# One queue's order at the opening of an MLP's down phase: loads of h and of weights in turn

## The chip, the cores and the metric

The kernel runs on one core of a Trainium2 chip. The metric is the device time of one execution in microseconds, the median of several runs. Three runs of the kernel before gave 2327.13, 2330.32 and 2327.13 us, so the median is 2327.13 us.

## What is computed

The reference is one inference step of a two-layer decoder (model width 1024, MLP width 4096, 1024 prompt tokens and 8 x 4 sample tokens, 1056 in all, all float32): an mLSTM layer and then a sliding-window attention layer. Each of the two ends in the MLP that this case is about:

```
def sq_relu_mlp(x, w_up, w_down):
    h = jax.nn.relu(x @ w_up)
    return (h * h) @ w_down
...
        x = x + sq_relu_mlp(rmsnorm(x, norm_ffn[l]), w_up[l], w_down[l])
```

## The kernel before

All five engines run instruction streams written by hand, tied together by semaphores. Each float32 operand of a matmul is split into a high part (ScalarE, a copy that rounds) and a low part (VectorE, the operand minus its high part), and three matmuls (high by high, high by low, low by high) make one product.

**The MLP.** The function `mlp` stands once for each engine, and `mlp_loads` (L777) is SyncE's part, the only one that issues the DMAs of weights and of h. The MLP's 4096 hidden rows are 16 blocks (NF) of 256. The up phase makes a block of h at a time and stores it to DRAM (`store_h`, L794). The down phase multiplies by w_down with a seven-product scheme (Strassen's, in a variant): the table DOWN names for each of the 7 products which half of the weights is summed with which other half, and which half of h with which other. A product runs over 7 groups (KG), so q runs from 0 to 48 (NG is 49), and a short tail follows (NW is 53 weight slabs). A group q is four pairs of output banks by 12 matmuls, 48 matmuls of 128x264 in all (L2765 to L2767).

**What a group needs.** `load_w(q)` (L803) loads a slab of weights into one of three places in turn (`w_raw`, `w_raw_odd`, `w_third`), and in the first product a second slab into one of two others; POOL adds the two (`down_sum`, L1499); ACT makes the high part (`w_high`, L1067); DVE makes the low part (`w_low`, L1669); only then may PE run group q. `load_h(q)` loads the group's part of h: for q = 0 to 6 into its own place in `b11` (L839), for q = 7 to 13 into `b21_even` or `b21_odd` (L848). ACT makes its high part (`t_high_of`, L1084) and DVE its low part (`t_low_of`, L1677), one group ahead of the weights.

**Waits ahead of the loads.** load_w(1) waits for the last split of the up phase (`op_lo`), load_w(2) for the store of block 14 (`h_stored`), load_w(q) from q = 3 for the low part of the weights of group q - 3 (`dw_lo`). The second slab of load_w(q) waits for POOL's sum of group q - 2 (`dw_sum`, L823, issue at L824). The first four h loads wait for a product of the up phase, and from the fifth on load_h(q) waits for the landing of load_h(q - 4) (`db_loaded`, L838). `store_h(15)` waits for the last two halves of h (`scaled`, L1663), which are worked out while the down phase is already under way; ACT's `stage` at the end of product 0 waits for this store, since it writes over the place where those halves lie.

**The order at the opening.** Each engine takes its instructions in the order in which they are written. At the end of the up phase DVE's order is: combine C11, U4, C22 (L1656, which read the accumulator), w_low(0), t_low_of(1), C21, C12, scaled(15, 1), w_low(1), t_low_of(2), scaled(15, 0), w_low(2), t_low_of(3) and so on. ACT's order is: t_high_of(0), w_high(0), t_high_of(1), relu and square of one half of block 15 (L1137, L1139), w_high(1), t_high_of(2), relu and square of the other half, w_high(2), t_high_of(3). PE's third and fourth bank pair of group 0 wait for C21 and C12. SyncE's order is the one that the change touches; all h loads of product 0 come first:

```
                for q in range(KG):
                    load_h(q)
                load_w(1)
                load_w(2)
                for q in range(3, NW):
                    if KG <= q + 1 < NG:
                        load_h(q + 1)
                    load_w(q)
                    if q == 4:
                        store_h(NF - 1)
```

Of the kernel before, what the change touches and what calls it, by code (L numbers as in the profile page):

```python
# [206 lines left out]
KG = (NF - TAIL) // 2  # L207
# [9 lines left out]
NG = NPROD * KG  # L217
# [12 lines left out]
def fill_no(layer, f, x):  # L230
    return UP_FILLS * layer + (2 * f + x + 1 if f < PLAIN else 2 * PLAIN + 7 * (f - PLAIN) + x + 1)


def up_no(layer, f, j):
    return UP_STEPS * layer + 7 * (f - PLAIN) + j + 1
# [6 lines left out]
def turns(layer, n, of, ring):  # L242

    return layer * len(range(n % ring, of, ring)) + n // ring + 1
# [6 lines left out]
def build(nc, io):  # L251
    with ExitStack() as ctx:  # L252
# [231 lines left out]
        def down_raw(q):  # L484
            return (w_raw[:, 0], w_raw_odd[:, 0], w_third[:])[q % 3]

        def down_other(n):
            return (w_raw, w_raw_odd)[n % 2][:, 1]
# [8 lines left out]
        def streamed(q):  # L497
            return (b21_even, b21_odd)[STREAMED.index(q) % 2]

        def down_h(q, half):  # L500

            if half == (1, 0):
                return streamed(q)[:]
            return {(0, 0): b11, (0, 1): b12, (1, 1): b22}[half][:, q % KG]
# [185 lines left out]
        def _(sp):  # L690
# [86 lines left out]
            def mlp_loads(layer):  # L777
# [16 lines left out]
                def store_h(f):  # L794
                    for c in (1, 0):
                        sp.wait_ge(zz_ready, 2 * (NF * layer + f) + 2 - c)
                        sp.dma_start(h_rows[layer][2 * f + c], z_of(f)[c]).then_inc(h_stored[f % 2], 16)

                def down_part(f, mh):
                    return down_rows[2 * P * f:2 * P * f + 2 * P, 512 * mh:512 * mh + 512].rearrange("(k p) m -> p k m", p=P)  # L800

                def load_w(q):

                    if q == 0:
                        sp.wait_ge(op_lo, fill_no(layer, NF - 2, 6))
                    elif q == 1:
                        sp.wait_ge(op_lo, fill_no(layer, NF - 1, 6))
                    elif q == 2:
                        sp.wait_ge(h_stored[0], 32 * (NF // 2) * (layer + 1))
                    else:  # L810
                        sp.wait_ge(dw_lo, NW * layer + q - 2)
                    if q < NG:
                        (mh, kh), op, other = DOWN[q // KG][0:3]
                        f = KG * kh + q % KG
                    else:
                        t, mh = TAILS[layer][q - NG]
                        f, op = NF - TAIL + t, None
                    sp.dma_start(down_raw(q).rearrange("p (k m) -> p k m", k=2), down_part(f, mh)).then_inc(dw_loaded[q % 3], 16)
                    if op is not None:
                        n = W_SUMS.index(q)  # L820
                        if n >= 2:
                            sp.wait_ge(dw_sum, len(W_SUMS) * layer + n - 1)
                        mh, kh = other  # L823
                        sp.dma_start(down_other(n).rearrange("p (k m) -> p k m", k=2), down_part(KG * kh + q % KG, mh)  # L824
                                     ).then_inc(dv_loaded[n % 2], 16)

                def load_h(q):

                    i, g = divmod(q, KG)
                    for half in LOADED_IN:  # L830
                        if LOADED_IN[half] == i:
                            n = RESIDENT.index((half, g))
                            kh, nh = half
                            f = KG * kh + g
                            sp.wait_ge(up_done, up_no(layer, NF - 1, (1 if g < 4 else 2) if half == (0, 0) else 6))
                            sp.wait_ge(h_stored[f % 2], 32 * ((NF // 2) * layer + f // 2 + 1))
                            if n >= 4:
                                sp.wait_ge(db_loaded[n % 4], 16 * (turns(layer, n, len(RESIDENT), 4) - 1))  # L838
                            sp.dma_start(down_h(q, half), h_rows[layer][2 * f:2 * f + 2, :, HALVES[nh]].rearrange("c p n -> p c n")  # L839
                                         ).then_inc(db_loaded[n % 4], 16)  # L840
                    if q in STREAMED:
                        n, f = STREAMED.index(q), KG + g
                        if n >= 2:
                            sp.wait_ge(dt_sum, len(T_SUMS) * layer + T_SUMS.index(STREAMED[n - 2]) + 1)
                        else:
                            sp.wait_ge(up_done, up_no(layer, NF - 1, 6))
                        sp.wait_ge(h_stored[f % 2], 32 * ((NF // 2) * layer + f // 2 + 1))
                        sp.dma_start(streamed(q)[:], h_rows[layer][2 * f:2 * f + 2, :, FIRST_H].rearrange("c p n -> p c n")  # L848
                                     ).then_inc(ds_loaded[n % 2], 16)

                def load_tail_h():
                    sp.wait_ge(dt_sum, len(T_SUMS) * layer + T_SUMS.index(last_group(3)) + 1)
                    for t in range(TAIL):
                        f = NF - TAIL + t
                        sp.wait_ge(h_stored[f % 2], 32 * (NF // 2) * (layer + 1))
                        for c in range(2):
                            sp.dma_start(h_raw[:, 2 * t + c], h_rows[layer][2 * f + c]).then_inc(ht_loaded, 16)
# [4 lines left out]
                for f in range(1, NF):  # L862
# [2 lines left out]
                        load_up(f + 2)  # L865
                    if f == NF - 2:
                        load_w(0)
                for q in range(KG):
                    load_h(q)
                load_w(1)  # L870
                load_w(2)
                for q in range(3, NW):
                    if KG <= q + 1 < NG:
                        load_h(q + 1)
                    load_w(q)
                    if q == 4:
                        store_h(NF - 1)
                    if q == 4 * KG + 4:
                        load_tail_h()

            mlp_loads(0)

            kv_w = io["w_kv"].rearrange("(k p) m -> p k m", p=P)
# [58 lines left out]
            for p, (kind, n) in enumerate(ATT):  # L942
# [22 lines left out]
                if p == 12:  # L965
                    load_sample_bias(1)
                    load_cache(1)
            mlp_loads(1)
            for t in range(NT):
                sp.wait_ge(yt_dve, t + 1)  # L970
# [2067 lines left out]
```

## Time and profile before

| what | value |
|---|---|
| median of three runs | 2327.13 us |
| the profiled execution | 2330.0 us |
| its span, first to last instruction | 2328.2 us |
| PE busy | 2253.5 us, 97% of the span |
| DVE busy | 1565.2 us, 67% |
| ACT, POOL busy | 1072.2 us, 46%; 501.8 us, 22% |
| granted TensorE clock, mean | 0.99 |

The profile is of one execution, 2.9 us above the median and inside the spread of the three runs. Times in the rows are microseconds from the start of the span unless a view says ns. PE is TensorE's matmuls, DVE VectorE, ACT ScalarE, POOL GpSimd, SPq the queue of SyncE, which issues the DMAs. Layer 0's MLP opens its down phase near 897 us and layer 1's near 1957 us.

### The profile page before, as it was taken

The page shows a single profiled execution, that of the slowest core. Times are in us where ns is not written, and L with a number is a line of the kernel's source. Part 1 is how long each engine was busy: PE and PEld are TensorE (multiplying, and loading weights), DVE is VectorE, ACT ScalarE, POOL GpSimd, SP SyncE. Part 2 cuts the span into 40 slices and gives each one's busy share as a digit, 9 for nine tenths or more (in the row PEclk, how much of TensorE's full clock was granted, in tenths as well). Part 3 has the DMA queues.
Part 4 walks back from the last instruction along what each step waited for, and adds up shares of the span by engine and source line. Part 5 has one row for each costly group of instructions (what it writes and reads, how often), then busy time and mean ns, then how long its engine had stood idle before and what let it go on. Part 6 is the DMA issues. An engine that isn't in the chain of part 4 may idle for free. (4 is left out here: it accounts for less than half of the span.)

```text
span 2328.2 us, 41472 instructions
## 1 busy us (share of the span) xinstructions
PE 2253.5 (97%) x16886; PEld 2151.6 (92%) x16886; DVE 1565.2 (67%) x2516; ACT 1072.2 (46%) x2058; POOL 501.8 (22%) x403
## 2 busy tenths in 40 slices
PE   8999999999999999999999999999999999999999
PEld 7989898888999999999999877869999999999998
DVE  7555555569765556788976666475855656798883
ACT  4233222245766664433423454254666664343435
POOL 1000000013222223113412011013122223123323
PEclk9999999999999999999999999999999999999999
DMA  4111121102233336655641312101233336665551
GB/s 131 37 51 57 50 70 41 41 25 65 93 97 107 111 111 239 229 193 200 197 140 49 97 32 53 31 16 46 83 104 110 109 95 224 226 224 188 181 174 75
DMA packets 220928, 256.28 MB, mean 110 GB/s; under 512 B 27687, under 2 KB 144340, under 8 KB 220708
## 3 DMA queue, kind: packets, MB, share of 16 engines
q1 hardware_dynamic: 220596, 253.61, 33.6%
q8 instruction: 135, 2.21, 0.4%
q14 instruction: 53, 0.43, 0.1%
q10 hardware_dynamic: 144, 0.02, 0.0%
HBM read 211.84 MB, written 46.93 MB: 111 GB/s over the span
## 5 line engine op out<-in xcount | busy, mean ns | idle before, releaser
L2765 PE MATMUL acc<-t_hi,w_hi 128*128 128x264 f32 x1568 | 450.5, 287 | 24.5 <-DVE w_lo L1669 24.5
L2766 PE MATMUL acc<-t_lo,w_hi 128*128 128x264 f32 x1568 | 450.8, 287 | 0.0
L2767 PE MATMUL acc<-t_hi,w_lo 128*128 128x264 f32 x1568 | 450.6, 287 | 0.0
L2765 PEld LDWEIGHTS acc<-t_hi,w_hi 128*128 128x128 f32 x1568 | 299.9, 191 | 27.9 <-DVE w_lo L1669 27.9
L2767 PEld LDWEIGHTS acc<-t_hi,w_lo 128*128 128x128 f32 x1568 | 298.7, 190 | 0.0
L2766 PEld LDWEIGHTS acc<-t_lo,w_hi 128*128 128x128 f32 x1568 | 298.5, 190 | 0.0
L2731 PE MATMUL acc<-x_lo,w_hi 128*128 128x264 f32 x896 | 254.6, 284 | 0.0
L2732 PE MATMUL acc<-x_hi,w_lo 128*128 128x264 f32 x896 | 254.5, 284 | 0.0
L2730 PE MATMUL acc<-x_hi,w_hi 128*128 128x264 f32 x896 | 254.4, 284 | 0.0
L2486 PE MATMUL acc<-x_hi,w_hi 128*128 128x352 f32 x576 | 193.1, 335 | 1.4 <-DVE pair L1958 1.4
L2730 PE MATMUL acc<-T_hi,w_hi 128*128 128x264 f32 x672 | 190.9, 284 | 0.2
L2731 PE MATMUL acc<-T_lo,w_hi 128*128 128x264 f32 x672 | 190.7, 284 | 0.0
L2732 PE MATMUL acc<-T_hi,w_lo 128*128 128x264 f32 x672 | 190.3, 283 | 0.0
L2488 PE MATMUL acc<-x_hi,w_lo 128*128 128x352 f32 x576 | 185.9, 323 | 0.0
L2487 PE MATMUL acc<-x_lo,w_hi 128*128 128x352 f32 x576 | 185.3, 322 | 0.0
L2730 PEld LDWEIGHTS acc<-x_hi,w_hi 128*128 128x128 f32 x896 | 168.8, 188 | 0.0
L2731 PEld LDWEIGHTS acc<-x_lo,w_hi 128*128 128x128 f32 x896 | 168.7, 188 | 0.0
L2732 PEld LDWEIGHTS acc<-x_hi,w_lo 128*128 128x128 f32 x896 | 168.4, 188 | 0.0
L1677 DVE TENSOR_TENSOR t_lo<-t_sum_of,t_hi 128x1056 fp32r<-128x1056 f32 x70 | 134.6, 1923 | 1.7
L2730 PEld LDWEIGHTS acc<-T_hi,w_hi 128*128 128x128 f32 x672 | 126.6, 188 | 0.7 <-DVE w_lo L1642 0.7
L2731 PEld LDWEIGHTS acc<-T_lo,w_hi 128*128 128x128 f32 x672 | 126.6, 188 | 0.0
L2732 PEld LDWEIGHTS acc<-T_hi,w_lo 128*128 128x128 f32 x672 | 126.1, 188 | 0.0
(396 smaller groups left out, 5700.6 us busy)
## 6 DMA issues: line engine op xcount, KB each, us to landing
w_raw<-in_w_down SPq DMA_DIRECT2D x72, 512.0 KB, 4.9
w_raw_odd<-in_w_down SPq DMA_DIRECT2D x70, 512.0 KB, 4.7
b<-h_rows SPq DMA_DIRECT2D x42, 528.0 KB, 6.1
w_third<-in_w_down SPq DMA_DIRECT2D x34, 512.0 KB, 4.3
h_rows<-z_even SPq DMA_DIRECT2D x32, 528.0 KB, 2.7
w_raw<-in_w_up SPq DMA_DIRECT2D x32, 512.0 KB, 4.5
w_raw_odd<-in_w_up SPq DMA_DIRECT2D x32, 512.0 KB, 5.1
w_raw<-in_w_mlstm_in SPq DMA_DIRECT2D x24, 512.0 KB
```

Source lines behind the costliest of these rows:

```text
L1677: V.tensor_tensor(lo[:], src, hi[:].bitcast(F32), ALU.subtract).then_inc(dt_lo, 1)
L2486: T.matmul(block_of(g), hi, mh[:, span(b)], start=(kk == 0), stop=False)
L2487: T.matmul(block_of(g), hi, ml[:, span(b)], start=False, stop=False)
L2488: x = T.matmul(block_of(g), lo, mh[:, span(b)], start=False, stop=(kk == n_k - 1))
L2730: T.matmul(out[:, q], hi[:, k], mh[:, k, v], start=(k == 0), stop=False)
L2731: T.matmul(out[:, q], hi[:, k], ml[:, k, v], start=False, stop=False)
L2732: x = T.matmul(out[:, q], lo[:, k], mh[:, k, v], start=False, stop=(k == 3))
L2765: T.matmul(out[:, h], hi[:, c, rows], mh[:, c, v], start=(g == 0 and c == 0), stop=False)
L2766: T.matmul(out[:, h], hi[:, c, rows], ml[:, c, v], start=False, stop=False)
L2767: x = T.matmul(out[:, h], lo[:, c, rows], mh[:, c, v], start=False, stop=(g == KG - 1 and c == 1))
```

## The change

SyncE's queue gets another order where the down phase opens, in both layers. h of groups 0 and 1, weights of group 1, h of 2, weights of 2, h of 3 and 4, weights of 3; from there h of group q + 1 and the weights of group q in turn. The store of block 15 of h comes after load_w(5) in place of load_w(4). The loads are the same, each with the waits it had, and no other engine's stream is changed.

```
@@ -865,15 +865,18 @@
                         load_up(f + 2)
                     if f == NF - 2:
                         load_w(0)
-                for q in range(KG):
-                    load_h(q)
+                load_h(0)
+                load_h(1)
                 load_w(1)
+                load_h(2)
                 load_w(2)
+                load_h(3)
+                load_h(4)
                 for q in range(3, NW):
-                    if KG <= q + 1 < NG:
+                    if 4 < q + 1 < NG:
                         load_h(q + 1)
                     load_w(q)
-                    if q == 4:
+                    if q == 5:
                         store_h(NF - 1)
```

## Rows read from the trace of the kernel before

**Rows 1.** PE's waits, whole span: who waited for whom, us, times, longest.
```profile
PE acc L2765 <- DVE w_lo L1669: 24.5, 16, 5.3
```
**Rows 2.** Timeline of PE, layer 0: start, us, engine, line, operation, idle before.
```profile
897.02 0.28 PE L2765 MATMUL acc<-t_hi,w_hi 128*128 128x264 f32 x1
...
902.76 0.28 PE L2767 MATMUL acc<-t_hi,w_lo 128*128 128x264 f32 x1
908.38 0.59 PE L2765 MATMUL acc<-t_hi,w_hi 128*128 128x264 f32 x1 [5.33 <-DVE w_lo L1669]
```
**Rows 3.** Timeline of POOL, layer 0.
```profile
901.89 2.36 POOL L1499 TENSOR_TENSOR w_raw_odd<-w_raw_odd 128x1024 f32<-128x1024 f32 x1 [21.55 <-DMA w_raw_odd<-in_w_down]
904.88 2.35 POOL L1499 TENSOR_TENSOR w_third<-w_third,w_raw 128x1024 f32<-128x1024 f32 x1 [0.63 <-DMA w_raw<-in_w_down]
908.03 2.54 POOL L1499 TENSOR_TENSOR w_raw<-w_raw,w_raw_odd 128x1024 f32<-128x1024 f32 x1 [0.79 <-DMA w_raw_odd<-in_w_down]
914.46 2.95 POOL L1499 TENSOR_TENSOR w_raw_odd<-w_raw_odd,w_raw 128x1024 f32<-128x1024 f32 x1 [3.89 <-DMA w_raw<-in_w_down]
```
**Rows 4.** Timeline of SyncE's queue, layer 0.
```profile
883.69 10.16 SPq L839 DMA_DIRECT2D b<-h_rows  x7
893.90 0.46 SPq L818 DMA_DIRECT2D w_raw_odd<-in_w_down  x1
...
908.76 0.47 SPq L824 DMA_DIRECT2D w_raw<-in_w_down  x1
```
**Rows 5.** Timeline of ACT, layer 0.
```profile
890.76 1.09 ACT L1084 ACTIVATE t_hi<-b 128x1056 fp32r<-128x1056 f32 x1 [4.57 <-DMA b<-h_rows]
...
899.31 1.09 ACT L1139 ACTIVATE act_b<-act_b 128x1056 f32<-128x1056 f32 x1
904.35 1.06 ACT L1067 ACTIVATE w_hi<-w_raw_odd 128x1024 fp32r<-128x1024 f32 x1 [3.95 <-POOL w_raw_odd L1499]
...
916.86 1.06 ACT L1067 ACTIVATE w_hi<-w_raw 128x1024 fp32r<-128x1024 f32 x1 [6.48 <-PE acc L2767]
...
922.73 1.06 ACT L1067 ACTIVATE w_hi<-w_raw_odd 128x1024 fp32r<-128x1024 f32 x1 [3.83 <-PE acc L2767]
```
**Rows 6.** Timeline of DVE, layer 0.
```profile
886.25 0.68 DVE L1642 TENSOR_TENSOR w_lo<-s_tmp,w_hi 128x512 fp32r<-128x512 f32 x1
...
895.15 1.22 DVE L1669 TENSOR_TENSOR w_lo<-w_raw,w_hi 128x1024 fp32r<-128x1024 f32 x1
896.29 1.25 DVE L1677 TENSOR_TENSOR t_lo<-b,t_hi 128x1056 fp32r<-128x1056 f32 x1
897.46 0.70 DVE L1656 TENSOR_TENSOR act_b<-act_b,acc 128x528 f32<-128x528 f32 x1
...
905.44 2.88 DVE L1669 TENSOR_TENSOR w_lo<-w_raw_odd,w_hi 128x1024 fp32r<-128x1024 f32 x1 [3.75 <-ACT w_hi L1067]
908.25 3.44 DVE L1677 TENSOR_TENSOR t_lo<-b,t_hi 128x1056 fp32r<-128x1056 f32 x1
...
913.91 1.25 DVE L1677 TENSOR_TENSOR t_lo<-b,t_hi 128x1056 fp32r<-128x1056 f32 x1
```
**Rows 7.** Stretches of layer 0: busy time by engine, then PEclk, DMA share, GB/s.
```profile
897.00:903.00 6.00, 6.00 (x50) 5.83 (x48) 3.02 (x4) 2.18 (x2) 1.10 (x1) 1.00 1.00 355
...
908.40:911.00 2.60, 2.60 (x12) 2.60 (x13) 2.60 (x1) 1.99 (x3) 2.17 (x1) 0.50 0.51 109
...
1097.90:1101.30 3.40, 3.40 (x17) 3.40 (x17) 3.32 (x4) 1.08 (x1) 0.00 (x0) 0.50 0.84 299
```
**Rows 8.** Timeline of PE, layer 1.
```profile
1957.34 0.28 PE L2765 MATMUL acc<-t_hi,w_hi 128*128 128x264 f32 x1
...
1968.37 0.59 PE L2765 MATMUL acc<-t_hi,w_hi 128*128 128x264 f32 x1 [5.00 <-DVE w_lo L1669]
```
**Rows 9.** Timelines of ACT, DVE and POOL, layer 1.
```profile
1949.07 1.09 ACT L1084 ACTIVATE t_hi<-b 128x1056 fp32r<-128x1056 f32 x1 [2.55 <-DMA b<-h_rows]
...
1976.01 1.06 ACT L1067 ACTIVATE w_hi<-w_raw 128x1024 fp32r<-128x1024 f32 x1 [5.29 <-PE acc L2767]
...
1953.79 1.22 DVE L1669 TENSOR_TENSOR w_lo<-w_raw,w_hi 128x1024 fp32r<-128x1024 f32 x1
...
1962.22 2.36 POOL L1499 TENSOR_TENSOR w_raw_odd<-w_raw_odd 128x1024 f32<-128x1024 f32 x1 [21.56 <-DMA w_raw_odd<-in_w_down]
```
**Rows 10.** Timeline of PE: two later pauses of the same kind, layer 0.
```profile
1096.53 0.39 PE L2765 MATMUL acc<-t_hi,w_hi 128*128 128x264 f32 x1 [2.33 <-DVE w_lo L1669]
...
1190.99 0.39 PE L2765 MATMUL acc<-t_hi,w_hi 128*128 128x264 f32 x1 [0.71 <-DVE w_lo L1669]
```

## Prediction

> **What bounds the kernel now.** I read the page first: PE is busy for 97% of the span, so a change can win only where PE stands still or runs at a lower clock. Then the list of PE's waits over the whole span: matmuls of the down phase waited 24.5 us in 16 pauses for the low part of the weights, and the longest was 5.3 us [rows 1]. PE's timeline places the longest: in layer 0 group 0 runs from 897.02 us, its last matmul starts at 902.76, and group 1 starts only at 908.38, after 5.33 us of idling [rows 2]. Layer 1 has the twin, 5.00 us, ahead of 1968.37 [rows 8]. Both lie where the changed lines act. The other 14 pauses come to 24.5 - 5.3 - 5.0 = 14 us and lie elsewhere.
>
> Followed backward, the pause is a chain. PE waited for w_low(1), 905.44 to 908.32 [rows 6]; that for w_high(1), which started at 904.35 after 3.95 us of waiting for POOL [rows 5]; POOL's sum started at 901.89 and had waited 21.55 us for a DMA [rows 3]; and that load was issued at 893.90, behind seven h loads whose issue had filled the queue from 883.69, 10.16 us [rows 4]. The first of these h loads lands at 890.7 (ACT starts on it at 890.76 [rows 5]), the second weight slab of group 1 at 901.85 (POOL's start [rows 3]). Eight transfers lie between, so one passes each 11.1 / 8 = 1.39 us, while the DMA engines are busy at share 1.00 [rows 7]. They are a line: a slab of weights lands when what stands ahead of it is through. In layer 1 the same reading gives (1962.2 - 1949.05) / 8 = 1.64 us a transfer [rows 9].
>
> **What the pause costs.** Matmuls follow each other at 5.86 / 48 = 0.122 us (group 0: 897.02 to 902.88) [rows 2]. Without the pause group 1 would start at 902.88 and end at 908.74. In fact ACT's w_high(3), released by the end of group 1, starts at 916.86 [rows 5]; the release comes some 0.45 us after the next group could start (an estimate: the last matmul starts 0.12 us before that point and itself takes 0.28, and the signal follows), so group 2 starts at about 916.4. The loss is 916.4 - 908.7 = 7.7 us: 5.5 of standing, 2.2 because the granted clock fell to 0.50 of full, the 1.2 GHz level, after the pause [rows 7]. Layer 1: group 0 from 1957.34, so with 5.87 us a group, the spacing of w_high(3) and w_high(4) [rows 5], group 2 could start at 1957.34 + 2 x 5.87 = 1969.1; it starts at 1976.01 - 0.45 = 1975.55 [rows 8, 9]; the loss is 6.5. Both together, 14.2 us, are the ceiling of the gain.
>
> **The change, part by part.**
>
> *Group 1's weights ahead of five h loads.* In layer 0 SyncE reaches load_w(1) after two h loads, at about 884.6, and waits for the last split of the up phase, done at 886.93 [rows 6]; both slabs are issued by 888, while h of groups 0 and 1 are still moving, so the line never runs dry. They are third and fourth transfers after the first: 890.7 + 3 x 1.39 = 894.9 against 901.85, seven us earlier. Nothing else queued is hurt by the wait of 2.3 us: the h loads behind it are needed from 901 on.
>
> *Where the time goes next.* POOL's sum of group 1 (2.36 us) now falls among DVE's steps. The rows show that two such operations exclude each other: t_low_of from 908.25 took 3.44 in place of 1.25 us, beginning beside a sum that ended at 910.57, and w_low(1) took 2.88 beside the one that ended at 907.23 [rows 3, 6]; the other way round the sum from 914.46 took 2.95, since t_low_of ran until 915.16. Whoever comes second waits until the first is through. The combines (L1656), which read the accumulator, I take as free of it. Replay of layer 0: the sum holds 894.9 to 897.3; w_low(0), which started at 895.15 [rows 6], is pushed behind it and ends at 898.5, so group 0 starts at 898.5, 1.5 late; t_low_of(1) to 899.6, C21 to 900.3; relu and square (2 x 1.09) to 902.5; w_high(1) to 903.5; DVE's scaled half to 903.7 and w_low(1) to 904.9. Group 0 ends at 904.35, group 1 starts at 904.95 and ends at 910.8. The sum of group 3 takes DVE's next turn, 904.9 to 907.3; t_low_of(2) to 908.5, the second scaled half to 909.7, w_low(2) to 910.9. Group 2 starts at 910.95 against 916.4: **gain 5.45**.
>
> Replay of layer 1: the weights land at 1949.05 + 3 x 1.64 = 1954.0, just after w_low(0) has begun at 1953.79 [rows 9], so it is t_low_of(1) that is held, to 1958.5, and group 0 starts on time. C21 to 1959.2, relu and square to 1961.4, w_high(1) to 1962.4, w_low(1) to 1963.8; group 1 1963.9 to 1969.75; the sum of group 3, t_low_of(2), the scaled half and w_low(2) run to 1969.7. Group 2 starts at 1969.8 against 1975.55: **gain 5.75**.
>
> *Clock.* The pauses left are 0.6 to 1.5 us. A pause of 2.33 us was followed by 3.4 us at clock 0.50, half of which, 1.7, is lost [rows 7, 10]; one of 0.71 has matmuls at the usual pace around it. I take 0 for those left; the other bound is 1.7 a layer.
>
> *h loads of groups 2 to 6 and of 7, later.* h(2) is fifth after the first, at 896.3, and needed by ACT at 903.5; h(3) and h(4) by 902; h(5) stands behind the second slab of group 3, whose wait (the sum of group 1) ends by 897.3; h(6) behind load_w(4), which waits for w_low(1) at 904.9: it lands near 911 and is needed near 922. Cost 0, with over 7 us of cover each. If the cover were gone, each late transfer would cost its 1.39.
>
> *store_h(15) one load later.* In the old order it stood ahead of load_w(5) and held it until the second scaled half; now load_w(5) goes first. ACT's stage needs the store only at the end of product 0, over 20 us on. Cost 0, gain 0.
>
> *Downstream.* All later steps wait on one another and on none by the clock, so PE's earlier end passes on. Sum: 5.45 + 5.75 = 11.2 us. Against the profiled execution 2330.0 - 11.2 = 2318.8; it stands 2.9 over the median, so the median becomes 2327.1 - 11.2 = **2316**.
>
> **Rivals.** *A: sums and DVE steps miss one another.* A few tenths decide in layer 0 (894.9 against 895.15), and POOL may take turns that DVE leaves free. Then the whole 14.2 is won: 2313. Against it: 9 us of DVE work and three sums must fit between 895 and 909.
>
> *B: the sum of group 4 comes just ahead of w_low(2).* Its slabs wait for w_low(1) (904.9, 1963.8). In the old order the slab issued at 908.76 was summed at 914.46, 5.6 later [rows 3, 4]; so the sum is ready near 910.9, just behind w_low(2), which starts at 909.7. Were it ready 1.2 us sooner, w_low(2) would wait 2.36 and end at 913; a pause of 2.4 also drops the clock, 1.7 more. That takes 4 us of a layer's gain: 2320 with one layer hit, 2324 with both. The Trainium skill speaks for this one: its page "DMA: Bandwidth & Descriptors", in the part on the cost of a DMA, gives a fixed 2.0 us and 436 KB per us (a fit made on another issuing path); an estimate from it for the two slabs is 2.0 + 1049 / 436 = 4.4 us, ready at 909.3, ahead of w_low(2). By that rule B holds in both layers, 2324; by the row it does not. The 5.6 us of the row decide for me, being the same loads on the same queue.
>
> *C: the change doesn't do what it says.* If the weights still land late, because SyncE stands in one of the waits moved ahead (the split, the store of block 14), nothing moves: 2327. The rows date both waits before 889, against it.
>
> *D: slower.* One mechanism, that of the exclusion, in its worst phase: the sums of groups 1, 3 and 4 each begin just ahead of w_low(0), (1) and (2). Each pushes PE by about 2.3 (1.7 at the first, which has 0.65 of slack), 6.4, and two pauses above 2 us cost 1.7 each: 9.8 a layer against 7.7 and 6.5 removed, so 5.4 slower: 2332.5. It decides only where all three meet; one has to come 1 us sooner and another later than the replay has it.
>
> **How the numbers follow.** Forecast as summed, 2313.5 to 2319: 0.52. A: 0.13. B, one layer or both, or a clock drop with it: 0.22. C, or gains and losses near balance: 0.08. D: 0.05. A measurement here tells about 0.2% (4.7 us) from no change, so faster means below 2322.5: 0.52 + 0.13 + 0.18 of B = 0.83. Same: 0.04 of B + 0.08 = 0.12. Slower 0.05. The range goes from 2311.5 (A, and the runs' own scatter) to 2323.5 (B in both), and leaves out some 0.04 below and 0.14 above.
>
> **What would show it.** PE's timeline should show the two 5 us pauses gone, with at most three pauses of 0.5 to 1.7 us at each opening, and clock 1.00 through 900 to 916. POOL's sum of group 1 should start near 895 and 1955, and DVE should show a stretched w_low(0) in layer 0 (about 3.4 us) and a stretched t_low_of(1) in layer 1. If a pause of over 2 us stands ahead of group 2, B is right; if POOL's sum still starts near 902, C. The later pauses of layer 0 [rows 10] should keep their length and come about 5.5 us sooner; if they grow, the gain is given back there and my step "downstream" is wrong.

## The result, and the profile after

| | kernel before | kernel after |
|---|---|---|
| median of seven runs | 2327.13 us (2322.89 to 2330.83) | 2316.38 us (2310.98 to 2318.28) |
| ratio, 95% interval | | 0.9947 (0.9933 to 0.9961) |
| profiled execution, its span | 2330.0, 2328.2 us | 2310.98, 2309.2 us |
| granted TensorE clock, mean | 0.990 | 0.996 |

The medians differ by 10.75 us; the ratio, made of runs side by side, is 12.3 us, between 9 and 15.6. The forecast was 2316 (2311.5 to 2323.5), faster by 11.2. In the profile after, L2768 is the matmul line that was L2765.

PE's waits over the whole span, the first line of the list (who waited for whom, us, times, longest), answer to [rows 1]:

```profile
PE acc L2768 <- DVE w_lo L1672: 14.3, 15, 2.9
```

24.5 us have become 14.3, and the two pauses of 5 us are gone. The same stretch as [rows 2], PE's timeline of layer 0, and layer 1's for [rows 8]: group 0 starts at 898.25, and no pause stands ahead of group 1. In layer 1 one of 0.37 us is left.

```profile
898.25 0.28 PE L2768 MATMUL acc<-t_hi,w_hi 128*128 128x264 f32 x1
...
1955.11 0.39 PE L2768 MATMUL acc<-t_hi,w_hi 128*128 128x264 f32 x1 [0.37 <-DVE w_lo L1672]
```

SyncE's queue, POOL and DVE of layer 0, for [rows 3, 4, 6]:

```profile
888.20 0.37 SPq L818 DMA_DIRECT2D w_raw_odd<-in_w_down  x1
888.62 0.46 SPq L824 DMA_DIRECT2D w_raw_odd<-in_w_down  x1
889.18 0.41 SPq L839 DMA_DIRECT2D b<-h_rows  x1
...
894.32 2.39 POOL L1502 TENSOR_TENSOR w_raw_odd<-w_raw_odd 128x1024 f32<-128x1024 f32 x1 [12.75 <-DMA w_raw_odd<-in_w_down]
...
909.76 2.44 POOL L1502 TENSOR_TENSOR w_raw_odd<-w_raw_odd,w_raw 128x1024 f32<-128x1024 f32 x1 [2.08 <-DMA w_raw<-in_w_down]
...
894.71 3.08 DVE L1672 TENSOR_TENSOR w_lo<-w_raw,w_hi 128x1024 fp32r<-128x1024 f32 x1
897.72 1.25 DVE L1680 TENSOR_TENSOR t_lo<-b,t_hi 128x1056 fp32r<-128x1056 f32 x1
...
903.03 1.22 DVE L1672 TENSOR_TENSOR w_lo<-w_raw_odd,w_hi 128x1024 fp32r<-128x1024 f32 x1
...
905.87 2.94 DVE L1666 TENSOR_TENSOR act_a<-act_a,rstd 128x1056 f32<-128x1056 f32 x1 [0.45 <-ACT act_a L1142]
908.73 1.21 DVE L1672 TENSOR_TENSOR w_lo<-w_third,w_hi 128x1024 fp32r<-128x1024 f32 x1
```

The weights of group 1 are issued at 888.20, ahead of the third h load, and POOL sums them from 894.32: 3.9 us before group 0 starts, where it was 4.9 us after. The low part of group 0's weights is stretched to 3.08 us beside this sum, as the replay had it. But it ends at 897.79, still 0.46 us before PE is free for it. The low part of group 1 is done at 904.25, within 0.15 us of the end of group 0's matmuls (898.25 + 5.87 = 904.1), so PE meets no visible pause.

ACT's w_high(3), released by the end of group 1, is the measure of the whole opening [rows 5]:

```profile
910.47 1.06 ACT L1070 ACTIVATE w_hi<-w_raw 128x1024 fp32r<-128x1024 f32 x1 [2.71 <-PE acc L2770]
...
1961.27 1.06 ACT L1070 ACTIVATE w_hi<-w_raw 128x1024 fp32r<-128x1024 f32 x1 [2.71 <-PE acc L2770]
```

From group 0's start it comes 910.47 - 898.25 = 12.22 us later in layer 0 (before: 916.86 - 897.02 = 19.84) and 12.55 in layer 1 (before: 18.67). The two openings gave 7.6 + 6.1 = 13.7 us between these two executions. The view of stretches, for [rows 7] (PE, PEld, DVE, ACT, POOL, then PEclk, DMA share, GB/s), shows the clock whole through both groups:

```profile
898.00:904.00 6.00, 6.00 (x52) 6.00 (x50) 4.34 (x5) 4.36 (x5) 2.45 (x1) 1.00 1.04 389
904.00:910.00 6.00, 5.97 (x49) 5.77 (x48) 5.55 (x5) 3.72 (x4) 3.51 (x2) 1.00 0.84 280
```

The spans differ by 19.0 us, more than 13.7. The before profile has five later drops to the 1.2 GHz level, each 3.4 us long and so at most 1.7 us dear: three in the down phases, one at 1418.8 and one at 2319.9. The after profile has none of them, but it reached group 0 of layer 0 1.2 us later. That makes 13.7 + 8.5 - 1.2 = 21.0 us, 2 more than measured, which I can't place. Such drops vary between executions of one kernel (the last experiment), so this part of the difference isn't put down to the change.

### The profile page after: what moved, and what is told of

It reads as the page before. It is cut to its first block and busy times, and to the rows that moved or that the text cites. A ratio compares the mean times of both kernels' runs of the same rounds, so it can differ in the third digit from the quotient of the medians.

```text
span 2309.2 us, 41472 instructions
## 1 busy us (share of the span) xinstructions
PE 2243.8 (97%) x16886; PEld 2141.8 (93%) x16886; DVE 1570.5 (68%) x2516; ACT 1072.1 (46%) x2058; POOL 500.3 (22%) x403
## 5 line engine op out<-in xcount | busy, mean ns | idle before, releaser
L2768 PE MATMUL acc<-t_hi,w_hi 128*128 128x264 f32 x1568 | 446.5, 285 | 14.3 <-DVE w_lo L1672 14.3
L2768 PEld LDWEIGHTS acc<-t_hi,w_hi 128*128 128x128 f32 x1568 | 295.9, 189 | 17.8 <-DVE w_lo L1672 17.7
L1680 DVE TENSOR_TENSOR t_lo<-t_sum_of,t_hi 128x1056 fp32r<-128x1056 f32 x70 | 127.8, 1826 | 1.7
```

Of the source, the lines that this page charges most:

```text
L1680: V.tensor_tensor(lo[:], src, hi[:].bitcast(F32), ALU.subtract).then_inc(dt_lo, 1)
L2768: T.matmul(out[:, h], hi[:, c, rows], mh[:, c, v], start=(g == 0 and c == 0), stop=False)
```

## Experiments

Every one was timed beside the kernel before. A ratio is given with its 95% interval, and as microseconds of 2326. For each opening I read two numbers: the pause ahead of group 1, and the opening's length from group 0's start to w_high(3). Its floor, with PE never waiting, is 11.92 us, found in both layers of the new order without the sums and in layer 1 of the old order without them.

### Group 1's weights alone moved

```
-                for q in range(KG):
-                    load_h(q)
+                load_h(0)
+                load_h(1)
                 load_w(1)
+                for q in range(2, KG):
+                    load_h(q)
                 load_w(2)
```

> Old order, but the weights of group 1 are loaded after the second h; h of 2 to 6 and then the weights of 2 follow, the store of block 15 stays after load_w(4). Line theory (a slab lands when the transfers issued ahead of it are through, 1.39 us each): POOL's sum of group 1 starts near 895 us and near 1953, so the 5 us pauses ahead of group 1 are gone (under 1 us); the sum of group 2 starts near 905 as before, and its weights' low part ends between 909.5 and 911 where group 2 could start at 909, so a pause of 0.7 to 2.3 us stands ahead of group 2 in each layer. Gain against the kernel before 8 to 12 us (the whole change: 10.8). Rival (only the store's place or the later loads matter): the pause ahead of group 1 stays at 5 us, gain 0.

Measured 0.9973 (0.9964 to 0.9983), 6.3 us gained, median 2320.34. The pauses ahead of group 1 are 0.32 and 0.36 us. Those ahead of group 2 came as forecast: PE's timeline in both layers, and POOL's second sum, which started only at 903.10 after 7.27 us of waiting for its load.

```profile
903.10 2.52 POOL L1501 TENSOR_TENSOR w_third<-w_third,w_raw 128x1024 f32<-128x1024 f32 x1 [7.27 <-DMA w_raw<-in_w_down]
...
911.31 0.39 PE L2767 MATMUL acc<-t_hi,w_hi 128*128 128x264 f32 x1 [1.75 <-DVE w_lo L1671]
...
1965.16 0.39 PE L2767 MATMUL acc<-t_hi,w_hi 128*128 128x264 f32 x1 [1.73 <-DVE w_lo L1671]
```

The pause follows the slab that is left behind the h loads. The gain, 6.3, lies under the 8 to 12 expected. Up to w_high(4), which comes after this pause, the two openings are 2.4 and 2.0 us longer than in the kernel after, 4.4 of the 6.0 us by which the gain falls short of the whole change's; the rest is within the intervals. No drop of the clock stands behind these pauses of 1.7 us.

### The store back in its old place

```
-                    if q == 5:
+                    if q == 4:
                         store_h(NF - 1)
```

> The kernel after with the store of block 15 of h moved back from behind load_w(5) to behind load_w(4). Line theory: the store holds load_w(5) until the second scaled half, near 908.8, about when load_w(5) is free to go anyway; no pause appears, the time is that of the kernel after within 2 us, so 9 to 13 us under the kernel before. Rival (the store's place carries part of the gain): a pause of over 1 us ahead of groups 2 to 5, the gain falls below 7 us.

Measured 0.9949 (0.9936 to 0.9963), 11.9 us, median 2315.34. The openings are 13.18 and 12.55 us, with pauses of 0.99 and 0.36 ahead of group 1 and none ahead of groups 2 to 5. The store's new place carries nothing of the gain.

### One layer at a time

```
+                if layer == 0:
                     load_h(0)
                     load_h(1)
                     load_w(1)
...
+                else:
+                    for q in range(KG):
+                        load_h(q)
+                    load_w(1)
+                    load_w(2)
```

(and with `layer == 1` in the second kernel)

> The new order in layer 0 alone, layer 1 keeps the old order. If the two layers' gains simply add, layer 0's part is its removed loss, 7.7 us less what is left of pauses: gain 5.5 to 7.7 us, with the 5.0 us pause of layer 1 in place and its clock drop of 3.4 us behind it. Rival (what layer 0 wins is lost again in the stages up to layer 1): gain under 3 us.

> The new order in layer 1 alone. With layer 0 alone the gain was 0.24%, 5.6 us. If the layers add, layer 1 alone gives what is left of the whole change's 10.5 to 11 us: 4.5 to 6.5 us, with the 5 us pause of layer 0 in place. Rival (the gain of one layer lies partly in fewer clock drops elsewhere): under 3 us or over 8.

Layer 0 alone: 0.9976 (0.9967 to 0.9985), 5.6 us. Layer 1 alone: 0.9971 (0.9963 to 0.9980), 6.7 us (4.7 to 8.6 by its interval), just above the 4.5 to 6.5 expected, a miss of no weight. Together 12.3 us, what the whole change gives by its ratio: within the intervals the gains add, and nothing is seen to be lost on the way. The changed layers have openings of 13.47 us (layer 0, with a pause of 1.28 ahead of group 1) and 12.93 us (layer 1, 0.74), somewhat longer than in the kernel after. In each kernel the layer left alone keeps its pause, but a smaller one than in the first profile. PE's timeline of layer 1 where layer 0 alone was changed, and of layer 0 where layer 1 alone was changed:

```profile
1962.12 0.39 PE L2782 MATMUL acc<-t_hi,w_hi 128*128 128x264 f32 x1 [4.15 <-DVE w_lo L1686]
```
```profile
906.49 0.39 PE L2782 MATMUL acc<-t_hi,w_hi 128*128 128x264 f32 x1 [3.18 <-DVE w_lo L1686]
```

### Four and six h loads ahead of the weights

```
-                load_w(1)
                 load_h(2)
+                load_h(3)
+                load_w(1)
                 load_w(2)
-                load_h(3)
                 load_h(4)
```

> The kernel after with four h loads ahead of the weights of groups 1 and 2 in place of two. Line theory: two more transfers, 2.7 us; the sum of group 1 starts near 898 and ends near 900.4, just before ACT is free for its high part, so no pause ahead of group 1 above 0.7 us; it begins after the low part of the weights of group 0, which keeps its 1.22 us in both layers. Time that of the kernel after within 2 us. Rival (every transfer ahead costs its 1.39 us): two pauses of 2.7 us or more, and the gain of 10.8 falls to 5 or less.

```
                 load_h(0)
                 load_h(1)
+                for q in range(2, 6):
+                    load_h(q)
                 load_w(1)
-                load_h(2)
                 load_w(2)
-                load_h(3)
-                load_h(4)
                 for q in range(3, NW):
-                    if 4 < q + 1 < NG:
+                    if 6 <= q + 1 < NG:
```

> The kernel after with six h loads ahead of the weights of groups 1 and 2. Line theory: four more transfers than after (two more than with four h); the second slab of group 1 lands 7 x 1.39 = 9.7 us after the first h, near 900.5, its low part ends near 905, a pause of about 2 us ahead of group 1 in each layer (old order 5.0 to 5.3, two or four h 0 to 1). Gain over the kernel before 6 to 10 us. Rival (the pause depends only on whether all h come first): pauses as in the kernel after, under 1 us, gain 11.

Four: 0.9963 (0.9949 to 0.9977), 8.6 us, median 2316.01, which by the median is the kernel after and by the ratio 3.7 us behind it, with openings 0.1 to 0.2 us longer; the difference is no larger than the intervals. Six: 0.9992 (0.9983 to 1.0001), 1.9 us, median 2324.67, far under the 6 to 10 us expected, and its interval reaches to no gain at all. POOL's first sum, in layer 0 of the one with four and of the one with six:

```profile
897.56 2.41 POOL L1502 TENSOR_TENSOR w_raw_odd<-w_raw_odd 128x1024 f32<-128x1024 f32 x1 [15.52 <-DMA w_raw_odd<-in_w_down]
```
```profile
902.30 3.02 POOL L1501 TENSOR_TENSOR w_raw_odd<-w_raw_odd 128x1024 f32<-128x1024 f32 x1 [19.47 <-DMA w_raw_odd<-in_w_down]
905.28 2.35 POOL L1501 TENSOR_TENSOR w_third<-w_third,w_raw 128x1024 f32<-128x1024 f32 x1
...
906.50 2.22 DVE L1671 TENSOR_TENSOR w_lo<-w_raw_odd,w_hi 128x1024 fp32r<-128x1024 f32 x1 [3.44 <-ACT w_hi L1069]
...
908.77 0.39 PE L2767 MATMUL acc<-t_hi,w_hi 128*128 128x264 f32 x1 [3.25 <-DVE w_lo L1671]
```

Set against group 0's start, in layers 0 and 1:

| h loads ahead | POOL starts the sum of group 1 | pause ahead of group 1 | opening |
|---|---|---|---|
| 2 (after) | 3.9, 3.1 us before it | 0, 0.37 us | 12.2, 12.6 us |
| 4 | 1.2, 0.5 before | 0.23, 0.47 | 12.4, 12.7 |
| 6 | 2.8, 2.9 after | 3.25, 3.04 | 17.0, 16.7 |
| 7 (before) | 4.9, 4.9 after | 5.33, 5.01 | 19.8, 18.7 |

Five h loads move the sum by 8.8 and 7.9 us, so 1.6 to 1.8 each, near the 1.39 and 1.64 of the forecast. The pause does not follow one for one. The first two extra transfers cost the openings 0.1 to 0.2 us, since POOL's sums hold DVE up once either way. With two h loads ahead it is the sum of group 1 (w_low(0) took 3.08 us), and ACT comes to w_high(1) only 3.5 us after group 0's start (901.72 - 898.25). With four, ACT is there 1.6 us after it, but DVE's step on the scaled half falls beside the sum of group 2, and w_low(1) starts 5.0 us after group 0's start, where it was 4.8. ACT and DVE, layer 0, with four:

```profile
900.32 1.04 ACT L1070 ACTIVATE w_hi<-w_raw_odd 128x1024 fp32r<-128x1024 f32 x1
```
```profile
900.45 3.33 DVE L1666 TENSOR_TENSOR act_b<-act_b,rstd 128x1056 f32<-128x1056 f32 x1 [0.76 <-ACT act_b L1142]
903.71 1.21 DVE L1672 TENSOR_TENSOR w_lo<-w_raw_odd,w_hi 128x1024 fp32r<-128x1024 f32 x1
```

From four on, each transfer lengthens the pause by 1.3 to 2.1 us. With six, the pauses of 3.25 and 3.04 are one more than I expected, and behind each the clock fell to 0.5 for 3.4 us, which I hadn't counted. The step that I had left out is in the rows: the next sum starts the moment that ACT has the first, and w_low(1) takes 2.22 us beside it in place of 1.22.

### POOL's sums taken out of product 0

```
-                nc.gpsimd.tensor_tensor(down_raw(q), down_raw(q), down_other(n), DOWN[q // KG][1]).then_inc(dw_sum, 1)
+                cols_of = slice(0, 8) if q < KG else slice(0, 1024)
+                nc.gpsimd.tensor_tensor(down_raw(q)[:, cols_of], down_raw(q)[:, cols_of], down_other(n)[:, cols_of],
+                                        DOWN[q // KG][1]).then_inc(dw_sum, 1)
```

> Leaves out most of POOL's sums in product 0 of both layers (8 of 1024 columns are summed), in the old order. POOL's 2.36 us and the 1.7 us by which the next sum stretches the low part fall out of the chain; the load stays late. Pauses ahead of group 1 fall from 5.3 and 5.0 to about 1.5 and 1.3; with the clock drops behind them gone as well the gain is 8 to 11 us. If instead the pause were the load alone, it would stay above 4 us.

> Leaves out most of POOL's sums in product 0 of both layers (8 of 1024 columns are summed), in the new order. If the exclusion of POOL and DVE costs nothing that PE sees in the kernel after, only the 0 and 0.4 us pauses at the opening go and the time is that of the kernel after within 2 us; the low part of the weights of group 0 takes 1.22 us in both layers. If the prediction's replay were right in what it charges to the exclusion (1.5 and 0.6 us in layer 0, 0.7 in layer 1), it would be 3 us faster.

In the old order: 0.9948 (0.9933 to 0.9963), 12.1 us, median 2314.79. The gain is above the 8 to 11 expected. No pause is left ahead of group 1 in either layer, where 1.5 and 1.3 us were expected; the openings are 11.99 and 11.92. The slab also came earlier here than in the first profile: POOL started 3.15 and 2.28 us after group 0, where it was 4.9 and 4.9. In the new order: 0.9948 (0.9933 to 0.9963), median 2313.33, openings 11.92 and 11.92.

Both kernels leave out 1016 of the 1024 columns of each sum of product 0, so they serve for their times alone. The one in the old order is best held against layer 0 of the kernel with layer 1 alone changed, which had the slab about equally early (POOL starts 2.99 us after group 0, against 3.15). The first two lines are the one with small sums, the last two the one with whole sums:

```profile
901.34 0.20 POOL L1500 TENSOR_TENSOR w_raw_odd<-w_raw_odd 128x8 f32<-128x8 f32 x1 [22.02 <-DMA w_raw_odd<-in_w_down]
...
902.73 1.23 DVE L1671 TENSOR_TENSOR w_lo<-w_raw_odd,w_hi 128x1024 fp32r<-128x1024 f32 x1 [1.55 <-ACT w_hi L1067]
```
```profile
900.28 2.38 POOL L1516 TENSOR_TENSOR w_raw_odd<-w_raw_odd 128x1024 f32<-128x1024 f32 x1 [19.67 <-DMA w_raw_odd<-in_w_down]
...
903.84 2.60 DVE L1686 TENSOR_TENSOR w_lo<-w_raw_odd,w_hi 128x1024 fp32r<-128x1024 f32 x1 [3.55 <-ACT w_hi L1084]
```

2.2 us less of sum and 1.4 less of stretched low part: 3.6 us, and the 3.18 us pause is gone. So a slab 3 us late is hidden by itself; it takes the load, the sum and the exclusion, one after another, to make the pause. For one 4.9 us late, as in the first profile, the same 3.6 us off the pause of 5.33 would leave 1.7 us (an estimate, in no run here). In the new order the ratio is that of the kernel after (0.9947, and 0.9949 in a second measurement). The median is 3 us lower, which by itself would fit the other expectation; the openings decide it: without the sums they are 0.3 to 0.8 us shorter, 0.9 to 1.4 us for both layers. That is what the exclusion still costs there, and not 3.

### Sums in two halves

```
-                nc.gpsimd.tensor_tensor(down_raw(q), down_raw(q), down_other(n), DOWN[q // KG][1]).then_inc(dw_sum, 1)
+                for part in (slice(0, 512), slice(512, 1024)):
+                    x = nc.gpsimd.tensor_tensor(down_raw(q)[:, part], down_raw(q)[:, part], down_other(n)[:, part],
+                                                DOWN[q // KG][1])
+                x.then_inc(dw_sum, 1)
```

> The kernel after with each of POOL's sums of weights as two instructions of 512 columns, in all products with sums. If DVE waits for whatever POOL instruction is running, its longest wait halves (3.45 us steps become about 2.4), the later pauses of 2.3 and 2.9 us fall to about 1.2 and 1.8, and with them the clock drops that follow pauses of that length: 2 to 7 us faster than the kernel after, 13 to 18 under the kernel before. Rival (POOL takes both halves in one go, or the second half costs DVE as much again): steps of 3.4 us stay and the time is that of after or up to 3 us slower.

Measured 0.9960 (0.9946 to 0.9973), 9.3 us, median 2316.20: no gain over the kernel after, where 2 to 7 us were expected. The expected shortening of each single wait came. DVE's steps beside a sum now take 2.3 us in place of 3.4, and the pauses of 2.3 and 2.9 us are 1.2 and 1.8, the longest. DVE's timeline:

```profile
1083.40 2.35 DVE L1710 TENSOR_TENSOR x_res<-x_res,act_a 128x1056 f32<-128x1056 f32 x1
1085.68 2.35 DVE L1703 TENSOR_TENSOR t_sum_of<-b 128x1056 f32<-128x1056 f32 x1
1087.95 2.31 DVE L1675 TENSOR_TENSOR w_lo<-w_third,w_hi 128x1024 fp32r<-128x1024 f32 x1
```

and the first line of PE's waits over the whole span:

```profile
PE acc L2771 <- DVE w_lo L1675: 13.1, 11, 1.8
```

But more steps are hit (three in a row here): about 120 of DVE's steps in the two down phases take over 1.6 us, where the kernel after has about 60. The sum of the pauses falls only from 14.3 to 13.1 us, and the mean granted clock of the five executions, 0.991 to 0.995, is no higher than the kernel after's, 0.992 to 0.996. Shorter turns of the same total leave the wait almost where it was.

### Both kernels once more

> The kernel before, profiled a second time. If the pauses of 5.3 and 5.0 us are a property of the order and not of one execution, they are there again, each between 3.5 and 6 us. The later clock drops (four of 3.4 us in the first profile) should differ in number, since the same pauses of 2.3 and 2.9 us were followed by a drop in one profile and by none in another.

> The kernel after, profiled and timed again. The opening pauses stay under 1.3 us in each layer. The first profile of it was one without any later clock drop, 2311.0 us against a median of 2316.4; another has one to three drops of 3.4 us, each costing 1.7 us. Gain over the kernel before 9 to 12 us.

Before: one run, 2331.2 us, pauses of 5.76 and 3.50 us, openings of 20.10 and 17.19. Layer 1's pause sits at the edge of the expected range. After: 0.9949 (0.9935 to 0.9963), 11.9 us, median 2317.43, pauses of 0.51 and 0.37, openings of 12.70 and 12.56.

The drops of the clock: in the kernel before the second profile has five later ones again, near the same places, one of them twice as long, so their number did not differ as expected. In the kernel after it did: the second profile has three that the first has not (at 454.5, 6.8 us long, at 1096.2 and at 1417.0). One pause shows it. PE's timeline and the stretch behind the pause (columns as above), in the first profile of the kernel after:

```profile
1090.14 0.39 PE L2768 MATMUL acc<-t_hi,w_hi 128*128 128x264 f32 x1 [2.31 <-DVE w_lo L1672]
```
```profile
1090.20:1093.60 3.40, 3.40 (x28) 3.40 (x29) 3.40 (x4) 0.00 (x0) 0.00 (x0) 1.00 0.69 189
```

and in the second:

```profile
1094.63 0.40 PE L2768 MATMUL acc<-t_hi,w_hi 128*128 128x264 f32 x1 [2.34 <-DVE w_lo L1672]
```
```profile
1096.20:1099.60 3.40, 3.40 (x18) 3.40 (x17) 3.32 (x4) 1.09 (x1) 0.00 (x0) 0.50 0.82 292
```

After 2.31 us of pause the clock stayed whole; after 2.34 us it fell to 0.50 for 3.4 us. In layer 1 of the first profile it stayed whole even after 2.91 us, where the kernel before has a pause of 2.90 us and 3.4 us at 0.50 from 2251.6:

```profile
2233.86 0.39 PE L2768 MATMUL acc<-t_hi,w_hi 128*128 128x264 f32 x1 [2.91 <-DVE w_lo L1672]
```
```profile
2233.90:2237.30 3.40, 3.40 (x28) 3.40 (x29) 2.38 (x2) 0.90 (x1) 0.00 (x0) 1.00 0.47 154
```

## Why the prediction was right, and where its steps were off

**The chain of the pause** held at each link. Moving the slab alone removes all but 0.3 to 0.4 us of the pause ahead of group 1; taking the sum out removes it too, where the slab is about 3 us late; and the number of transfers ahead sets when the sum starts.

**The ceiling, 14.2 us, was too high**, since it came from one execution. The old order's openings were 19.84, 20.10 and 16.87 us in layer 0 (before, before again, layer 1 alone changed) and 18.67, 17.19 and 17.87 in layer 1 (before, before again, layer 0 alone changed). Their means, 18.9 and 17.9, lie 7.0 and 6.0 over the floor of 11.92: the ceiling is 13.0 us. How far POOL's sum came after group 0's start moved by 2.7 us between executions of the same order.

**What is left after the change was put too high**, by about as much. The replay had group 2 of layer 0 at 910.95, an opening of 14.4 us counted from the old start of group 0, 1.5 of it from the step "group 0 starts 1.5 late"; it is 12.2 and 12.7 in the two profiles of the kernel after, and 13.5 where layer 0 alone was changed. That step failed. I took w_low(0)'s start of 895.15 as fixed, 1.87 us before group 0, and put the sum just ahead of it. In the first profile of the kernel after, the sum does come first, but w_low(0) starts 3.5 us before group 0 and the 1.86 us that the sum adds are covered. In the second profile, and where layer 0 alone was changed, the sum starts 0.2 and 0.1 us after w_low(0), which takes its usual 1.22 us; t_low_of(1) is the step that is held, as in my replay of layer 1, and a pause of 0.51 and 1.28 us stands ahead of group 1. POOL and DVE of layer 0, second profile:

```profile
899.06 3.25 POOL L1502 TENSOR_TENSOR w_raw_odd<-w_raw_odd 128x1024 f32<-128x1024 f32 x1 [13.51 <-DMA w_raw_odd<-in_w_down]
```
```profile
898.84 1.22 DVE L1672 TENSOR_TENSOR w_lo<-w_raw,w_hi 128x1024 fp32r<-128x1024 f32 x1
899.98 3.45 DVE L1680 TENSOR_TENSOR t_lo<-b,t_hi 128x1056 fp32r<-128x1056 f32 x1
```

w_low(0) comes behind t_low_of(0) and so behind the first h load, on which ACT started 6.26 us before group 0 in the profile before, against 8.11, 7.77 and 7.00 in these three. Whether the new order makes the first h load earlier or it merely was in those runs is open: the old order had it 6.3, 6.3 and 8.0 us ahead. Layer 1's replay gave an opening of 12.9; it is 12.55, 12.56 and 12.93.

Together, over three executions of each order: 18.9 + 17.9 less 12.8 + 12.7 is 11.4 us by the openings, 12.3 by the ratio, 10.75 by the medians, 11.2 forecast. Two errors of 1.2 and 1.4 us with opposite signs cancelled (a ceiling of 13.0 for 14.2, and 1.6 left over for 3.0), so that the size came out this close is in part luck; the path and the removal of both pauses are not.

**Hidden costs.** The later h loads and the store cost nothing, as forecast. **Downstream**, the gain was passed on: the single-layer gains add, and the pauses outside the openings came to 14.3 - 0.4 = 13.9 us against 24.5 - 10.3 = 14.2, with 2.31 for 2.33 and 2.91 for 2.90 among them. The first pause of [rows 10] came 6.4 us sooner, the opening's 7.6 less the later start of 1.2. The second, 0.71 us, has no twin; a pause of 1.69 stands at 1182.99, and the second profile of the kernel before has one of 1.69 at 1193.60 too, so it isn't of the new order. **Clock**: with pauses under 0.6 us in the two after profiles no drop stands at the openings, but one stood at each of the six old ones.

**Rivals.** *A* describes the first after profile best in its pauses, though the sums and steps did meet: the meetings fell where PE had slack. *B* did not occur: in the profile after, the sum of group 4 is ready at 909.76, about 1 us after w_low(2) has begun, 5.1 us after its load's issue at 904.68. By the Trainium skill's "DMA: Bandwidth & Descriptors", section "Anatomy of one DMA — SWDGE (gpsimd) path", whose fit is 2.0 us and 436 KB per us, an estimate for both slabs is 4.4 us after the first slab's issue at 904.27, so 908.7, just as w_low(2) starts; the trace, 5.5 us, doesn't agree, and the row of the same loads was the better guide. *C* is refuted by POOL's early start, *D* by the openings.

## What to carry to other kernels

Where one queue feeds several consumers, write the loads in the order in which the steps that need them fall due, counting each step's own preparation: here weights need a sum, a high and a low part (6 us), h only the latter two. Two transfers too many ahead cost almost nothing and four put a pause of 3 us into each layer, so look for the slack before moving more. And measure a pause in more than one execution before taking it as the ceiling: here it moved by 1.5 to 2.6 us in a layer.

## What was not expected of the hardware

- A pause of 2.3 us of PE was followed by a drop to the 1.2 GHz level in one execution (2.34 us, then 0.50 for 3.4 us) and not in another (2.31 us, clock 1.00), nor was one of 2.91. Each drop costs up to 1.7 us, and the spread between runs of one kernel goes with them: the kernel after took 2310.98 and 2311.39 us at a mean clock of 0.996, and 2318.28 at 0.992. Its two profiles, 2309.2 and 2316.3 us of span, have nearly equal pauses in the down phases (14.3 and 15.5 us), and the longer has three drops more.
- Where a POOL sum and DVE steps contend, POOL gets its turn after the running DVE instruction, even with DVE's next one waiting: in the rows of the second profile above, the sum of 2.4 us that starts 0.2 us after w_low(0) is through in 3.25, and it is t_low_of(1) that takes 3.45 for 1.25. Cutting POOL's instruction in two halves each wait (3.45 to 2.35 us) and hits more DVE steps: pauses 13.1 for 14.3 us, no gain in time.
